# Operands of the fp32r products moved to other places modulo 512 bytes in SBUF, and a smaller DMA scratch for GpSimd

## The reference

```
for l in range(2):                      # first block
    x = x + norm(mix(norm(x) @ w_in[l]) @ w_out[l])
    gate, up = split(norm(x) @ w_ffn_in[l])           # 1024 -> 2 * 2816
    x = x + norm((silu(gate) * up) @ w_ffn_out[l])    # 2816 -> 1024
for l in range(2):                      # second block
    x = x + 0.5 * swiglu(norm(x), w1[l], w2[l])
    x = x + (merge of three branches of norm(x) @ w_in_2[l]) @ w_out_2[l]
    x = x + 0.5 * swiglu(norm(x), w1b[l], w2b[l])
return norm(x)
```

## Time and profile before

| | |
|---|---|
| median of 3 runs | 3474.77 us (3471.44 to 3475.7) |
| the profiled execution | 3470.74 us, its span 3468.9 us |
| TensorE matmul busy | 3365.4 us, 97% of the span, 19557 matmuls |
| TensorE weight load busy | 2884.7 us, 83% |
| VectorE, ScalarE, GpSimd busy | 71%, 47%, 2% |
| granted TensorE clock | 0.994 of full speed |

### The profile page before, as it was taken

One profiled execution on the slowest core, in us unless ns is written; L12 is line 12 of the kernel. 1 busy time (PEld: TensorE's weight loads), 2 busy tenths in 40 slices (PEclk: granted clock), 3 DMA queues, 4 the chain that ended last, 5 costly groups with the idle time before them and its releaser, 6 DMA issues.

```text
span 3468.9 us, 49474 instructions
## 1 busy us (share of the span) xinstructions
PE 3365.4 (97%) x19557; PEld 2884.7 (83%) x19557; DVE 2462.7 (71%) x3512; ACT 1617.0 (47%) x2387; POOL 55.9 (2%) x84
## 2 busy tenths in 40 slices
PE   7999999999999999999999999999999989999999
PEld 5678988767998799887687899889988767788997
DVE  8669854759882888557895698559864888658863
ACT  4645543455562466326524356425542562335642
POOL 1000000000000000000000000000000000000000
PEclk9999999999999999999999999999999999999999
DMA  4123323212332233232133233323333213322332
GB/s 141 50 73 98 99 97 109 82 49 82 102 114 99 76 113 110 95 104 60 49 91 91 97 98 110 100 94 98 110 104 97 75 44 90 92 97 86 110 104 85
DMA packets 339642, 318.95 MB, mean 92 GB/s; under 512 B 31768, under 2 KB 312164, under 8 KB 339428
## 3 DMA queue, kind: packets, MB, share of 16 engines
q1 hardware_dynamic: 335588, 307.95, 28.0%
q0 software_dynamic: 2048, 6.16, 0.5%
q10 hardware_dynamic: 1792, 1.88, 0.2%
HBM read 313.84 MB, written 2.10 MB: 91 GB/s over the span
## 4 chain that ended last, share of the span: by engine, by line
PE 80%; DVE 15%; ACT 3%; issue 2%; DMA 0%; POOL 0%; DVEq 0%; POOLq 0%
PE products L797 31%; PE products L938 24%; PE products L836 7%; PE small L836 6%; PE small L938 4%; PE products L1199 2%; DVE w_lo L2152 2%; DVE seven_x L2404 1%; PE products L1396 1%; DVE conv L2939 1%; DVE X L2172 1%; DVE x_sums L2393 1%; ACT w_hi L1522 1%; PE small L1273 1%; DVE mla_prob L2599 1%
## 5 line engine op out<-in xcount | busy, mean ns | idle before, releaser
L2152 DVE TENSOR_TENSOR w_lo<-raw,w_hi 128x2048 fp32r<-128x2048 f32 x190 | 435.1, 2290 | 482.7 <-ACT w_hi L1522 482.4
L1522 ACT ACTIVATE w_hi<-raw 128x2048 fp32r<-128x2048 f32 x190 | 363.8, 1915 | 833.1 <-PE products L797 579.8
L797 PE MATMUL products<-a_hi,w_hi 128*128 128x512 f32 (+1 forms) x1216 | 490.8, 404 | 12.8 <-DVE a_lo L2212 10.1
L797 PE MATMUL products<-a_hi,w_lo 128*128 128x512 f32 (+1 forms) x1216 | 477.0, 392 | 0.0
L797 PE MATMUL products<-a_lo,w_hi 128*128 128x512 f32 (+1 forms) x1216 | 476.4, 392 | 0.0
L938 PE MATMUL products<-seven_x,w_hi 128*128 128x256 f32 x2592 | 465.6, 280 | 8.3 <-DVE w_lo L2433 3.2
L938 PEld LDWEIGHTS products<-seven_x,w_hi 128*128 128x128 f32 x2592 | 395.0, 188 | 12.2 <-DVE w_lo L2433 4.4
L938 PE MATMUL products<-seven_x,more_hi 128*128 128x256 f32 x1632 | 375.9, 279 | 3.6 <-ACT rs_b L1631 3.6
L938 PE MATMUL products<-seven_x,w_lo 128*128 128x256 f32 x1296 | 361.6, 279 | 0.0
L797 PEld LDWEIGHTS products<-a_hi,w_hi 128*128 128x128 f32 (+1 forms) x1216 | 229.9, 189 | 70.0 <-issue 16.7
L938 PEld LDWEIGHTS products<-seven_x,more_hi 128*128 128x128 f32 x1632 | 277.7, 188 | 4.8 <-ACT rs_b L1631 4.8
(11 more groups left out here) (463 smaller groups left out, 7228.8 us busy)
## 6 DMA issues: line engine op xcount, KB each, us to landing
raw<-in_ffn_w SPq DMA_DIRECT2D x244, 512.0 KB, 4.1
raw<-in_w_in SPq DMA_DIRECT2D x108, 512.0 KB, 4.6
raw<-in_w_ffn_in SPq DMA_DIRECT2D x88, 512.0 KB, 4.2
raw<-in_w_ffn_out SPq DMA_DIRECT2D x40, 512.0 KB, 4.5
raw<-in_w_out SPq DMA_DIRECT2D x32, 512.0 KB, 4.2
raw<-in_ffn_w SPq DMA_DIRECT2D x24, 384.0 KB, 3.5
raw<-in_w_mem_kv SPq DMA_DIRECT2D x8, 512.0 KB, 4.1
raw<-in_lru_w_out SPq DMA_DIRECT2D x8, 512.0 KB, 3.4
```

What stands on the lines that cost most here:

```text
L797: mm = pe.matmul(G[pair][0:m, into + b, 0:n], w[:, s, at:at + m], x, start=(first or into > 0) and k == 0 and q == 0, stop=(last or ends) ...
L1522: act.activation(w_hi[:, s, :], raw[:, s, :], ACT.Copy).then_inc(hi_ready, 1)
L2152: dve.tensor_tensor(w_lo[:, s, :], raw[:, s, :], w_hi[:, s, :].bitcast(F32), ALU.subtract).then_inc(lo_ready, 1)
```

## The change

It adds `onward(at, residue)`, which rounds an offset up to the next one with that residue modulo 512, and gives each region of operands a residue of its own, the same for the high and the low part. Sizes, shapes, instructions and their order stay. The scratch goes from 8192 to 4096 bytes, and everything behind it moves down by 4096 bytes, a multiple of 512.

```diff
-ODD = 32
+    def onward(at, residue):
+
+        return -(-(at - residue) // LINE) * LINE + residue
...
-    W_HI = top[0]
+    top[0] = W_HI = onward(top[0], 0)
...
-    REGION_A = top[0]
+    top[0] = REGION_A = onward(top[0], 256)
     a_hi = place("a_hi", [P, DC, SEQ], F32R)
+    top[0] = A_LO = onward(top[0], 256)
     a_lo = place("a_lo", [P, DC, SEQ], F32R)
...
+    MORE = onward(REGION_A, 448)
+    MORE_LO = onward(MORE + 10 * KB, 448)
+    LATE = onward(MORE_LO + 10 * KB, 64)
+    top[0] = REGION_B = onward(max(top[0], LATE + 12 * KB), 128)
+    SEVEN = onward(REGION_B, 64)
     h_hi = place("h_hi", [P, FC, SEQ], F32R)
...
+    top[0] = H_LO = onward(max(top[0], SEVEN + 44 * KB), 128)
     h_lo = place("h_lo", [P, FC, SEQ], F32R)
+    EARLY = onward(H_LO + 32 * KB, 0)
...
-    seven_x = place("seven_x", [P, 11, 4 * HALF], F32R, at=REGION_B + ODD)
-    late_hi = place("late_hi", [P, 3, 4 * HALF], F32R, at=REGION_A + 20 * KB + ODD)
-    more_hi = place("more_hi", [P, 5, QUAD], F32R, at=REGION_A)
+    seven_x = place("seven_x", [P, 11, 4 * HALF], F32R, at=SEVEN)
+    late_hi = place("late_hi", [P, 3, 4 * HALF], F32R, at=LATE)
+    more_hi = place("more_hi", [P, 5, QUAD], F32R, at=MORE)
...
-    b1[0] = REGION_B
+    b1[0] = YC = onward(REGION_B, 64)
...
+    b1[0] = onward(b1[0], 192)
+    YA = b1[0]
...
+    b1[0] = onward(b1[0], 320)
...
-    REGION_T = b1[0]
+    b1[0] = REGION_T = onward(b1[0], 384)
+    MG_LO = onward(REGION_T + 16 * KB, 384)
...
-    nc = _bacc.Bacc("TRN2", target_bir_lowering=False, num_devices=1, dynamic_dma_scratch_size=8192)
+    nc = _bacc.Bacc("TRN2", target_bir_lowering=False, num_devices=1, dynamic_dma_scratch_size=4096)
```

More of the change, by code:

```diff
@@ L290, in two_blocks @@
     raw = place("raw", [P, 2, UNIT])
-    W_HI = top[0]
+    top[0] = W_HI = onward(top[0], 0)
     w_hi = place("w_hi", [P, 2, UNIT], F32R)
-    W_LO = top[0]
+    top[0] = W_LO = onward(top[0], 0)
     w_lo = place("w_lo", [P, 2, UNIT], F32R)
@@ L298, in two_blocks @@
                 for i, at in enumerate((W_LO + 4 * UNIT, W_HI + 4 * UNIT, BROADCASTS, BROADCASTS + 4 * ROWS_4))]
-    REGION_A = top[0]
+    top[0] = REGION_A = onward(top[0], 256)
     a_hi = place("a_hi", [P, DC, SEQ], F32R)
+    top[0] = A_LO = onward(top[0], 256)
     a_lo = place("a_lo", [P, DC, SEQ], F32R)
     dft = place("dft", [P, TC // 2, 2, SEQ], at=REGION_A)
-    ab = place("ab", [P, TC, SEQ], at=REGION_A + 16 * KB)
+    ab = place("ab", [P, TC, SEQ], at=A_LO)
     rows = place("rows", [P, n_param_tiles, P], at=REGION_A)
     out_tok = place("out_tok", [P, TC, D], at=REGION_A)
-    top[0] += LINE
-    REGION_B = top[0]
+    MORE = onward(REGION_A, 448)
[3 more added lines that the diff above has]
+    SEVEN = onward(REGION_B, 64)
     h_hi = place("h_hi", [P, FC, SEQ], F32R)
-    top[0] += LINE
-    H_LO = top[0]
+    top[0] = H_LO = onward(max(top[0], SEVEN + 44 * KB), 128)
     h_lo = place("h_lo", [P, FC, SEQ], F32R)
+    EARLY = onward(H_LO + 32 * KB, 0)
+    top[0] = EARLY + 12 * KB
+    top[0] += 2 * LINE
     x_tok = place("x_tok", [P, TC, D], at=REGION_B)
@@ L316, in two_blocks @@
     QUAD = 4 * P
-    seven_x = place("seven_x", [P, 11, 4 * HALF], F32R, at=REGION_B + ODD)
-    late_hi = place("late_hi", [P, 3, 4 * HALF], F32R, at=REGION_A + 20 * KB + ODD)
-    more_hi = place("more_hi", [P, 5, QUAD], F32R, at=REGION_A)
[L320 to L325, removed]
+    seven_x = place("seven_x", [P, 11, 4 * HALF], F32R, at=SEVEN)
+    late_hi = place("late_hi", [P, 3, 4 * HALF], F32R, at=LATE)
+    more_hi = place("more_hi", [P, 5, QUAD], F32R, at=MORE)
+    more_lo = place("more_lo", [P, 5, QUAD], F32R, at=MORE_LO)
+    early_hi = place("early_hi", [P, 3, QUAD], F32R, at=EARLY)
+    early_lo = place("early_lo", [P, 3, QUAD], F32R, at=EARLY + 6 * KB)
+    more_sums = place("more_sums", [P, 5, QUAD], at=MORE_LO)
+    early_sums = place("early_sums", [P, 3, QUAD], at=EARLY + 6 * KB)
+    x_sums = place("x_sums", [P, 11, 4 * HALF], at=SEVEN)
     h_full = place("h_full", [P, FC, SEQ], at=H_LO)
@@ L404, in two_blocks @@
           for name in ("window", "rot_q", "dup0", "rot_k0", "dup1", "rot_k1", "dft_cos", "dft_sin")}
+    b1[0] = onward(b1[0], 0)
     m_hi = in_b("m_hi", [P, DC, MEM], F32R)
@@ L422, in two_blocks @@
     lru_in = in_b("lru_in", [P, LC, SEQ])
-    glu = place("glu", [P, LC, SEQ], at=REGION_B)
-    conv = place("conv", [P, LC, SEQ], at=REGION_B + 8 * KB)
+    glu = place("glu", [P, LC, SEQ], at=YC)
+    conv = place("conv", [P, LC, SEQ], at=YC + 8 * KB)
     craw_sq = place("craw_sq", [P, 5, SEQ], at=REGION_T)
[L426 to L429, removed]
+    lru_tmp = place("lru_tmp", [P, 3, SEQ], at=YA + 10 * KB)
+    craw = place("craw", [P, 6, SEQ], at=YA + 16 * KB)
+    gate_w = place("gate_w", [P, LC, 2, P], at=YA + 28 * KB)
+    mla_prob.append(place("mla_prob4", [P, ROWS_4], at=YA + 18 * KB))
     mla_prob.append(place("mla_prob5", [P, ROWS_4], at=REGION_T))
@@ L433, in two_blocks @@
     kv_head = place("kv_head", [P, MLA_HEADS, SEQ], at=REGION_T + 16 * KB)
-    v_head = place("v_head", [P, TC, MLA_HEADS * HEAD], at=REGION_T + 32 * KB)
+    v_head = place("v_head", [P, TC, MLA_HEADS * HEAD], at=MG_LO + 16 * KB)
     mg_hi = place("mg_hi", [P, DC, SEQ], F32R, at=REGION_T)
-    mg_lo = place("mg_lo", [P, DC, SEQ], F32R, at=REGION_T + 16 * KB)
-    partial = place("partial", [P, DC, SEQ], at=REGION_T + 16 * KB)
+    mg_lo = place("mg_lo", [P, DC, SEQ], F32R, at=MG_LO)
+    partial = place("partial", [P, DC, SEQ], at=MG_LO)
     def place_of(r):
```

## The result

The changed kernel took 3504.19 us (median of 3 runs, 3501.89 to 3505.99) against 3474.77 before: ratio 1.0087, 95% interval 1.0064 to 1.0109. It is slower by 29.4 us, where 58 us of gain were forecast. The profiled execution took 3505.99 us, its span 3504.2.

What follows compares the result with a forecast made beforehand. TensorE's matmul pace was taken to bound the kernel; 30.2 us (256 columns) plus 28.2 (512 columns) made 58.4 us off 3474.8, so 3416 us. Range 3375 to 3512, likeliest case 3375 to 3455.

Steps and rivals of the forecast that it cites:

- What bounds the kernel: TensorE's matmul chain: 226.7 ns per 512-column product in L797 and L836, 116.7 per 256-column product in L938.
- the room that VectorE had: VectorE, busy 85% of an L938 stage, would reach 88% if TensorE sped up; costed at 0.
- That the place matters: Matmul pace depends on operand places: 120.0 against 116.7 ns at 256 columns, 231.7 against 226.7 at 512.
- The 512-column term: L797, L836, L1199, L1396: 3.33 ns gained on each of 8460 products, 28.2 us.
- the mixed unit: Unit with 160-column rows, stationary slices at 0, 128, 256, 384 in turn, moving operand at 0: 231.7 ns per matmul.
- the 43 us of that bound: Worst case for the 512-column products: 231.7 ns each, 5.0 ns lost on 8556 products.
- The 256-column term: L938, moving operand from 32 to 64: 116.7 to 113.3 ns on 9072 products, 30.2 us gained.
- The bound of 112 to 113 ns: Floor for L938 if loads alone set the pace, from L871's one-column matmuls; at most 43 us gained.
- The scratch at 0: Halving GpSimd's scratch costs nothing; 43 us lost if each issue waited for the landing before.
- Rival 1: 512-column products fall out of step, 5.0 ns each, +43 us: 3518, or 3487 with L938's gain; chance 0.31 with mixes and scratch.
- rival 2: No change, 3475 us; chance 0.14.
- rival 3: Faster, to 3340 us; chance 0.08.

Runs made afterwards that it cites:

- kernel 5: Changed kernel with 512-column products back at distance 0 and all seven 256-column products at 192: 3453.44 us, ratio 0.9937 to the kernel before.
- kernel 7: Changed kernel with h, y and mg at 256 like a, seven products left at 64 and 448: 3482.45 us, ratio 1.0028 to the kernel before.
- kernel 8: Changed kernel with seven_x and late_hi back at 32 and more at 0: 3494.28 us, ratio 1.0064 to the kernel before.
- kernel 11: Kernel before with h_lo at 128 while h_hi stays at 0: 3488.9 us, one run.
- kernel 2: Changed kernel with operands at 128, seven_x and late_hi at 160, so distances are those of the kernel before: 3476.47 us, ratio 1.0003 to that kernel.
- kernel 1: Kernel before with only the scratch cut from 8192 to 4096 bytes: 3473.05 us, ratio 0.9992.
- the sweeps: Changed kernel with other places, so each operand tries a distance of its own: 3516.66 and 3518.45 us, one run each.
- sweep 1: Changed kernel with other distances, among them a 32, h 96, seven products 96 and 192 against more: 3516.66 us, one run.
- kernel 12: As the run with the seven products at distance 192 and all else at 0, but at 448: 3468.40 us, ratio 0.9976 to the kernel before.

## Why the prediction was wrong

**What bounds the kernel: right.** TensorE is busy for 97% of the span and makes up 80% of the chain, and its pace inside the runs of products moved the time, 33.6 of the 35.4 us between the traces; the waits of the earlier trace rows and VectorE's times stayed, and the room that VectorE had was never needed.

**That the place matters: right,** and shown by kernels 5, 7, 8 and 11; kernel 2 shows that it does so by the distance. The load and the stream run side by side (in a stage of the seven products loads are busy for 177.4 and matmuls for 178.5 of 183 us), but the pace hangs on their distance: from 113.3 to 120 ns with 256 columns, 226.7 to 234 with 512.

**The 512-column term: the step that failed.** "I have one point at 32 bytes and a mixture at 128 and more, and carry the first over to all the rest." The 28.2 us are 3.33 ns for each of 8460 products, the step from 120.0 to 116.7, and those two rows are of another length: no run shows such a gain with 512 columns. At 256 columns the step from distance 0 to 32 happens to gain 3.3 ns, since 0 is the slowest distance there; at 512 columns 0 is, with 256, the fastest (226.7), and the step to 32 costs 6.6. The row of the right length was there, the mixed unit's 231.7 ns, and I weighed it down because its distance changes. The term was forecast at -28.2 us and measured about +21: 20.3 between the traces from start to start, 20.7 and 21.7 by kernels 8 and 7 (the windows of busy time have 18.3). It comes from the products on and by h, and a little from mg and y. That it isn't the 43 us of that bound is luck: a, with 256, landed on the other good distance.

**The 256-column term: wrong too.** "I take another 3.3 ns, the step that the first 32 bytes gave." Pace over distance isn't monotone: 119.6, 116.7, 117.7, 119.4, 118.9 ns at 0, 32, 64, 96, 128. I named that as what would make the prediction wrong, and put no price on it. Forecast -30.2 us, measured +13.3 between the traces and +9 to +10 by the medians. The bound of 112 to 113 ns, from 0.34 us for three matmuls of one column, was good: the fastest pace found is 113.3.

**The scratch at 0: right** (kernel 1).

**The rivals.** Rival 1 (out of step) names the mechanism of the larger half, at 3487 to 3518 us; 3504 lies inside. Its point against itself, "it may show the changing and not the distance", was half right: kernel 11 shows that changing is enough, and the sweeps that a constant distance does it too. Its price of 5.0 ns was low by 0.7 to 1.6 ns on h. It counted all 8556 matmuls, where only about 4100 (1584 on h and 1584 by h, 384 on mg, 576 on y) left the even distances, and it had the 256-column products unchanged or 30 us faster, where they lost 9 to 13. So 3504 falls between its two times by luck, as the sum of half its loss and one that it didn't have. The chance of 0.14 for rival 2 went to no change, 3475 us, and the 0.08 for rival 3 to 3340 us; 3504 is neither.

**What stays open.** Why a given distance has the pace that it has, and what picks one of two lasting paces at a wait, isn't explained. VectorE's and ScalarE's operands moved along with TensorE's, and no run moved them alone; so a share of theirs in the loss isn't excluded. The border in sweep 1 speaks against it: there the pace goes from 119.2 to 113.0 ns from one matmul to the next, where only TensorE's own operand changes. Nor did a run take the load away and keep the stream, so it isn't shown that the two get in each other's way.

## What to carry to other kernels

For dense fp32r products, measure the pace at the real length of the moving operand for each distance between moving and stationary operand, modulo 256 bytes; a good distance at 256 columns says nothing for 512 (192: 113.3 ns, the fastest, but at 512 columns 233.4). An even pace isn't a good one by itself: both lengths are even at distance 0, where 512 columns are at their fastest (226.7 ns) and 256 at their slowest (119.6 to 120.0). Read the pace from a piece of the chain (us by count), or from start to start, and not from busy time, which grew by 5.6 us in L850 where the starts of the products on h show 8.9.

## What was new about the hardware

- Six of the paces lie close to one raster: 113.3 (kernel 5), 120.0 (memory tokens), 226.7 (h, before) and 233.3 ns (h, changed kernel) are 17, 18, 34 and 35 times 6.67 ns; 116.7 is 17.5 times and 117.8 is 17.67 times. Why 6.67 isn't shown. Some of them are even from start to start (226 or 227 at distance 0, 117 to 119 in the slow stages of kernel 5), and some are means of a pattern (229 and 238 ns in turn for 233.3 on h in the changed kernel).
- The same code at the same places has two lasting paces: 113.3 and 117.8 ns at distances 192 and 448 (kernels 5 and 12), 116.7 and 117.8 at 32 (kernels 1, 2 and 11). Each stage keeps the one that it had after its last wait, for some 160 us. At 192 a slow stage costs 6 us (1512 matmuls at 117.5 ns instead of 113.4), and it looks like noise from outside: 3440 to 3459 us for one kernel. Not all of such a spread is the two paces: the kernel before took from 3468.41 us at a granted clock of 0.996 to 3485.27 at 0.990.
- Distances nearly repeat every 256 bytes, not only every 512, wherever both were tried. With 512 columns 256 is as good as 0 (226.8 and 226.7 ns), 288, 320 and 352 do as 32, 64 and 96 within 0.1 ns, 416, 448 and 480 as 160, 192 and 224 within 0.4, and 384 is 0.9 off 128. With 256 columns 288 does as 32 (116.9 and 116.7), and 448 is as two-paced as 192 (113.5 and 117.6 ns against 113.4 and 117.5).
